# Inverting the triangular matrices of a delta-rule kernel: the first two doubling levels replaced by a back substitution on VectorE

## The chip, the cores and the metric

The kernel runs on one core of a Trainium2 chip. The metric is device time in microseconds of one execution. The medians are taken over several runs; one more execution is recorded by the hardware profiler.

## The reference

The reference is a small network on 512 tokens of width 1024. It has two hybrid layers (a gated delta rule with 8 heads, a windowed attention with 16 query heads and an MLP each) and one further block with a state space branch. The change is in the delta rule. Per head and per chunk of 64 tokens it solves with a unit lower triangular matrix:

```python
L = jnp.where(strict, jnp.einsum('bhnid,bhnjd->bhnij', kb, k) * decay, 0.0)
u = lax.linalg.triangular_solve(L, v * beta[..., None], left_side=True,
                                lower=True, unit_diagonal=True)
w = lax.linalg.triangular_solve(L, kb * jnp.exp(g)[..., None], left_side=True,
                                lower=True, unit_diagonal=True)
# then, chunk after chunk
v_new = u_c - jnp.einsum('bhcd,bhde->bhce', w_c, state)
o = (jnp.einsum('bhcd,bhde->bhce', qd, state) + jnp.einsum('bhij,bhje->bhie', a_c, v_new))
state = state * jnp.exp(gl)[..., None, None] + jnp.einsum('bhcd,bhce->bhde', kd, v_new)
```

All arithmetic is float32.

## The kernel before

**Weights.** Every product with a weight matrix is cut into tiles of 128 output columns by 1024 input rows (`LT_TILES`). A tile is loaded by SyncE, split by ScalarE (L909) and GpSimd (L916) into a high and a low part, and multiplied by TensorE in 24 matmuls of 128x512 (L946 to L948). In the order of work a tile is cut into 8 pieces of three matmuls. The outputs alternate between two PSUM banks, so VectorE has to evict a tile (L1712 for most) before the next but one can start.

**Inverse.** The kernel works with 128x128 blocks, each holding two chunks of 64 tokens; four blocks (`CH`) cover 512 tokens. A block of the transposed matrix lies in `LTm`. `XB` holds, for the lower and the upper 64 partitions, the transposed inverse of each chunk's own 64x64 matrix. It starts from 2x2 diagonal blocks: `first` copies the elements above the diagonal of each 2x2 block from `LTm`, `minus` subtracts them from the unit matrix (L1551, L1553). Then five doubling levels (`LEVELS` = 2, 4, 8, 16, 32) join blocks of that size. A level is a round trip between VectorE and TensorE: `flip` transposes 32x32 blocks of `XB` into `Xi` (L1568), `p` multiplies `LTm` with `Xi` (L1881), `pmask` cuts the result to the off-diagonal blocks of the level (L1572), `q` multiplies again (L1885), and `update` subtracts from `XB` (L1576). Behind the last level `turn`, `plast` and `qlast` join the two chunks of a 128x128 block into `XT`.

**Stages and order.** The work of a layer is a set of chains of stages. Chain D prepares a head: the squares and sums of q and k, the turned copies of k and v, decays, the two Gram products (L1862) and their masking into `LTm` (`maskk`, L1547) and `AT` (`maskq`, L1542). `first` and `minus` are stages of D between `maskk` and `gramq`. D runs through all eight heads one after another, and all its TensorE results go through one PSUM bank, `psD[:, 0]`, which is bank 2. Chain A holds the inverse's levels, head after head. Chains B (two lanes) hold the scan over the chunks. E holds the tiles' evictions and convolutions (`tap3` to `tap0`, `silu`), and C the windowed attention. Each stage waits for the count of its chain's semaphore. Among the waits between chains are these: `tap3` of the q tile of head h waits for the end of D of head h-2, A of a head waits for `minus` of the same head, and the first query tile of the windowed attention (`qraw`) waits for the last head's D and for the scan of the fourth and fifth last head. B of a head needs that head's A and D. Tile `ya` needs all heads.

**Who decides the order.** Each engine executes its instructions in the order in which a small planner (`ordered`, L278) emits the stages. The planner starts the stage that can start earliest by a table of assumed durations (`micros`, L339) times a factor (`slack1`, L375: 1.25 for stages of ScalarE, VectorE and GpSimd of the first six heads). This order is worked out when the kernel is built and is the same in each execution.

Of the kernel before, what the change touches and what calls it, by code (L numbers as in the profile page):

```python
# [9 lines left out]
ALU = mybir.AluOpType  # L10
# [15 lines left out]
SWAP = [i + ROT if i < ROT else i - ROT if i < 2 * ROT else i for i in range(32)]  # L26
LEVELS = (2, 4, 8, 16, 32)
BLK = 64
# [62 lines left out]
for _name, _n in [("ident", P), ("ones", P), ("invfreq", 1), ("isrot", 1), ("signrot", 1), ("notrot", 1),  # L91
                  ("eps", 1), ("eps4", 1), ("halfpi", 1), ("invcount", 16),
                  ("upper", P), ("first", BLK), ("later", P), ("levels", BLK * len(LEVELS)), ("unit", BLK),
                  ("dup0", P), ("dup1", P), ("window", 2 * P)]:
    CONST[_name] = (_at, _at + _n)
    _at += _n
# [22 lines left out]
def constants():  # L119
# [4 lines left out]
    def put(name, v):  # L124
        c[:, CONST[name][0]:CONST[name][1]] = v
# [4 lines left out]
    ib, jb = i % BLK, np.arange(BLK)[None, :]  # L130
    put("first", (ib % 2 == 0) & (jb == ib + 1))
    put("unit", ib == jb)
    put("later", np.where(i <= j, 0.0, NEG))
# [56 lines left out]
def e_stages(tile):  # L190
# [3 lines left out]
    if kind == "f2":  # L194
# [9 lines left out]
D_STAGES = ["square", "sums", "qscale", "turnk", "ksum", "root", "copyk", "turnv", "recip", "dscale", "copyv", "rows", "diff", "exps",  # L204
            "qdec", "gramk", "maskk", "first", "minus", "gramq", "maskq"]

# [132 lines left out]
def micros(e):  # L339
# [13 lines left out]
    if (kind, name) == ("Z", "double"):  # L353
        return (0.5, 1.2, 2.4, 3.0, 4.8, 3.6, 7.2)[int(s[len(name):])]
    special = {("N", "highs"): 2.5, ("N", "adds"): 3.0, ("A", "update"): 0.45, ("A", "turn"): 0.6, ("A", "p"): 1.1, ("A", "q"): 1.1, ("A", "plast"): 0.6, ("A", "qlast"): 0.6,
# [322 lines left out]
def build(nc, xT, pos, consts, gain0, params, weights, params2, smallbc, uD, yD, matsD, lagsD, outT):  # L678

    with ExitStack() as ctx:  # L680
# [92 lines left out]

        scal = sb("scal", [P, HEADS, 8, CH])
        srows = sb("srow", [P, 2, 4, CH])
        DSUM, DROOT, DRECIP, DCOL, DQ = range(5)
# [5 lines left out]
        ps = ctx.enter_context(nc.psum_tensor("ps", [P, 8, 512], F32))  # L782
        psD, psB, psA = ps[:, 2:4, :], ps[:, 4:6, :], ps[:, 6:8, :]
        psS = [ps[:, 4, 0:P], ps[:, 7, 0:P]]
        psO = [ps[:, 5, :], ps[:, 3, :]]
# [132 lines left out]

        def part(layer, earlier):
            names = ("tile_stage", "key_stage", "gate_stage", "gram_stage", "inverse_stage", "scan_even", "scan_odd", "window_even", "window_odd", "mlp_even", "mlp_odd",  # L920
                     "coef_stage", "x_ready", "sq_done", "h_high", "h_low", "ssq_done", "root_done", "rstd_ready", "x_scaled", "post_col", "pre_col", "pre_row",
                     "pre_sum", "sq_added", "post_sum", "coef_in", "sum_done", "post_root", "post_ready", "out_done", "setup", "out_ready", "state_stage", "y_stage",
                     "branch_even", "branch_odd", "mats_out", "mats_even", "mats_odd", "u_out", "u_even", "u_odd", "y_out", "y_in")
            (tile_stage, key_stage, gate_stage, gram_stage, inverse_stage, scan_even, scan_odd, window_even, window_odd, mlp_even, mlp_odd,
             coef_stage, x_ready, sq_done, h_high, h_low, ssq_done, root_done, rstd_ready, x_scaled, post_col, pre_col, pre_row,
             pre_sum, sq_added, post_sum, coef_in, sum_done, post_root, post_ready, out_done, setup, out_ready, state_stage, y_stage,
             branch_even, branch_odd, mats_out, mats_even, mats_odd, u_out, u_even, u_odd, y_out, y_in) = [sem(f"{n}{layer}") for n in names]

# [190 lines left out]

            steps = [0]  # L1120
            MATS_BEFORE, MATS_EACH = 16 * (3 * SG + 2 * SG), 16 * 5
# [145 lines left out]
            if layer < DEPTH:  # L1267
# [219 lines left out]
                def run_vector(v):  # L1487
                    for kind, j, s in L_ORDERS[layer]:
# [5 lines left out]
                        elif kind == "G":  # L1494
# [27 lines left out]
                            ins.then_inc(gate_stage, 1)  # L1522
                        elif kind == "D" and s in ("qscale", "recip", "dscale", "diff", "maskk", "maskq", "first", "minus"):
                            h = j
# [18 lines left out]
                            elif s == "maskk":  # L1543
                                if h >= 3:
                                    v.wait_ge(inverse_stage, A.end(GROUP_OF[h - 3]))
                                for c in range(CH):
                                    ins = v.scalar_tensor_tensor(out=lt[:, c, :], in0=a0[:, c, :], scalar=w[:, DCOL, c:c + 1],  # L1547
                                                                 in1=DT[:, c, :], op0=ALU.mult, op1=ALU.mult)
                            elif s == "first":
                                for b in (lower, upper):  # L1550
                                    ins = v.tensor_tensor(XB[b, (h + 1) % 4, :, :], lt[b, :, b], over_chunks(k_("first")[b], CH, BLK), ALU.mult)  # L1551
                            else:
                                ins = v.tensor_tensor(XB[:, (h + 1) % 4, :, :], over_chunks(k_("unit")), XB[:, (h + 1) % 4, :, :], ALU.subtract)  # L1553
                            ins.then_inc(gram_stage, 1)
# [853 lines left out]
```

## Time and profile before

| | us |
|---|---|
| median of 3 runs | 2500.5 (2500.2 to 2500.54) |
| the profiled execution, device time | 2497.98 |
| its span in the trace | 2496.2 |
| TensorE busy in it | 2414.7 |
| VectorE busy in it | 1266.1 |
| ScalarE busy in it | 1047.8 |
| GpSimd busy in it | 1152.0 |

PE is TensorE's matmuls, PEld its weight loads, DVE VectorE, ACT ScalarE, POOL GpSimd. Times in the trace are microseconds from the start of the span. A float32 matmul of the inverse and of the heads' work appears as two records, so a "p" or "q" step, four blocks by two halves of the partitions, is 16 records. The ends of matmuls are modelled, and a matmul's duration overlaps with the next one's start. The page has the totals; views of groups by line, of stretches of time and of instructions in order of time were read beside it.

### The profile page before, as it was taken

How to read it: one execution, taken by the hardware profiler on the slowest of the kernel's cores; microseconds unless marked ns; L12 is line 12 of the kernel's file. 1: busy time of each engine (PE TensorE's matmuls, PEld its weight loads, DVE VectorE, ACT ScalarE, POOL GpSimd, SP SyncE). 2: the span in 40 equal slices, each digit the busy share in tenths (PEclk: the TensorE clock that was granted, in tenths of full speed). 3: DMA queues.
4: the chain of work that ended last, by engine and by line, in shares of the span. 5: the costliest groups of instructions: out<-in, count | busy, mean ns of one | idle time of the engine just before them, and what ended most of it. 6: DMA issues, size and time to landing. Idle time of an engine off the chain costs nothing.

```text
span 2496.2 us, 35065 instructions
## 1 busy us (share of the span) xinstructions
PE 2414.7 (97%) x13972; PEld 1921.3 (77%) x13972; DVE 1266.1 (51%) x2172; ACT 1047.8 (42%) x2248; POOL 1152.0 (46%) x848
## 2 busy tenths in 40 slices
PE   7999999999999999989999999999999999799998
PEld 5787777778778888767877777787777788677886
DVE  4777744663341111286766446634586511566453
ACT  6565643443343323354656334533533232323342
POOL 4333323335666556543333233256665564433464
PEclk9999999999999999999999999999999999888999
DMA  4211112222323332311111122223133332362322
GB/s 147 60 52 60 52 43 64 65 75 77 101 68 95 100 93 93 101 51 60 60 52 52 43 77 68 60 90 120 61 114 121 120 93 93 112 175 85 101 93 76
DMA packets 76515, 207.48 MB, mean 83 GB/s; under 512 B 16704, under 2 KB 27712, under 8 KB 75840
## 3 DMA queue, kind: packets, MB, share of 16 engines
q1 hardware_dynamic: 76352, 205.24, 26.7%
q8 instruction: 111, 1.82, 0.3%
q14 instruction: 52, 0.43, 0.1%
HBM read 194.72 MB, written 10.49 MB: 82 GB/s over the span
## 4 chain that ended last, share of the span: by engine, by line
PE 83%; DVE 8%; ACT 4%; POOL 2%; issue 2%; DMA 1%; SPq 1%; DVEq 0%; ACTq 0%; POOLq 0%
PE ps L946 24%; PE ps L948 22%; PE ps L947 22%; PE ps L1881 2%; PE ps L1885 2%; PE ps L1934 1%; PE ps L1946 1%; PE ps L1862 1%; ACT wH L909 1%; POOL wL L916 1%; PE ps L1940 1%; DVE ctw L1156 1%; ACT prob L1419 1%; DVE ctmp L1156 1%; PE ps L1911 1%
## 5 line engine op out<-in xcount | busy, mean ns | idle before, releaser
L916 POOL TENSOR_TENSOR wL<-raw,wH 128x512 fp32r<-128x512 f32 x660 | 900.4, 1386 | 1151.7 <-ACT wH L909 1151.4
L909 ACT ACTIVATE wH<-raw 128x512 fp32r<-128x512 f32 x660 | 379.9, 624 | 760.0 <-PE ps L948 756.4
L946 PE MATMUL ps<-hH,wH 128*128 128x512 f32 x1592 | 667.0, 419 | 3.9 <-DVE mixed L2177 2.2
L948 PE MATMUL ps<-hH,wL 128*128 128x512 f32 x1592 | 631.9, 397 | 0.0
L947 PE MATMUL ps<-hL,wH 128*128 128x512 f32 x1592 | 630.0, 396 | 0.0
L946 PEld LDWEIGHTS ps<-hH,wH 128*128 128x128 f32 x1592 | 303.1, 190 | 74.0 <-issue 11.3
L948 PEld LDWEIGHTS ps<-hH,wL 128*128 128x128 f32 x1592 | 302.7, 190 | 67.6
L947 PEld LDWEIGHTS ps<-hL,wH 128*128 128x128 f32 x1592 | 304.2, 191 | 54.0 <-issue 0.5
L946 PE MATMUL ps<-OH,wH 128*128 128x512 f32 x576 | 230.8, 401 | 4.9 <-DVE acc L1741 1.8
L948 PE MATMUL ps<-OH,wL 128*128 128x512 f32 x576 | 227.8, 396 | 0.0
L947 PE MATMUL ps<-OL,wH 128*128 128x512 f32 x576 | 227.8, 395 | 0.0
L946 PE MATMUL ps<-SH,wH 128*128 128x512 f32 x436 | 172.6, 396 | 0.0
L948 PE MATMUL ps<-SH,wL 128*128 128x512 f32 x436 | 172.5, 396 | 0.0
L947 PE MATMUL ps<-SL,wH 128*128 128x512 f32 x436 | 172.4, 395 | 0.0
L946 PEld LDWEIGHTS ps<-OH,wH 128*128 128x128 f32 x576 | 108.2, 188 | 36.8 <-issue 9.2
L1743 DVE TENSOR_TENSOR acc<-acc,ps 128x512 f32<-128x512 f32 x48 | 33.1, 689 | 202.0 <-PE ps L948 202.0
L948 PEld LDWEIGHTS ps<-OH,wL 128*128 128x128 f32 x576 | 108.2, 188 | 26.0
L947 PEld LDWEIGHTS ps<-OL,wH 128*128 128x128 f32 x576 | 108.3, 188 | 24.8
L946 PEld LDWEIGHTS ps<-SH,wH 128*128 128x128 f32 x436 | 81.9, 188 | 20.2 <-issue 0.4
L948 PEld LDWEIGHTS ps<-SH,wL 128*128 128x128 f32 x436 | 81.9, 188 | 19.7
L947 PEld LDWEIGHTS ps<-SL,wH 128*128 128x128 f32 x436 | 81.9, 188 | 19.7
L1419 ACT ACTIVATE prob<-prob,small 128x256 f32<-128x256 f32 (+1 forms) x128 | 59.8, 469 | 61.6 <-DVE small L1657 61.6
(405 smaller groups left out, 3461.3 us busy)
## 6 DMA issues: line engine op xcount, KB each, us to landing
raw<-w SPq DMA_DIRECT2D x345, 512.0 KB, 3.5
mats<-matsD SPq DMA_DIRECT2D x4, 1408.0 KB, 6.7
x<-xT SPq DMA_DIRECT2D x8, 256.0 KB, 5.7
matsD<-Cd SPq DMA_DIRECT2D x8, 256.0 KB, 2.8
matsD<-wide SPq DMA_DIRECT2D x4, 512.0 KB, 3.6
mats<-lagsD SPq DMA_DIRECT2D x32, 64.0 KB, 6.7
outT<-acc SPq DMA_DIRECT2D x8, 256.0 KB, 2.2
matsD<-tab SPq DMA_DIRECT2D x8, 128.0 KB, 1.8
```

What stands on the lines that cost most here:

```text
L909: act.activation(weights_at(slot)[0][:, k, :], raw[:, n % RAW, k, :], ACT.Copy).then_inc(high_done, 1)
L916: pool.tensor_tensor(low[:, k, :], raw[:, n % RAW, k, :], high[:, k, :].bitcast(F32), ALU.subtract).then_inc(low_done, 1)
L946: pe.matmul(out, wh, rH[:, t, :], start=(t == 0), stop=False)
L947: pe.matmul(out, wh, rL[:, t, :], start=False, stop=False)
L948: mm = pe.matmul(out, wl, rH[:, t, :], start=False, stop=(t == depth - 1))
L1156: return v.tensor_tensor(o, a, b, ALU.mult)
L1419: act.activation(prob[:, i, a:], prob[:, i, a:], ACT.Exp, bias=nm4[:, i:i + 1], accum_out=den[:, i:i + 1])
L1743: ins = v.tensor_tensor(acc[:, i % 8, :], acc[:, i % 8, :], b, ALU.add)
L1862: ins = pe.matmul(psD[:, 0, cc], k[:, cc], (k if s == "gramk" else q)[:, cc], start=True, stop=True)
L1881: ins = pe.matmul(psA[b, 0, cc], lt[b, c, b], Xi[b, i, :], start=True, stop=True)
L1885: ins = pe.matmul(second_half(psA[b, 0, cc], n), Pm[b, i, :], second_half(xb[b, i, :], n), start=True, stop=True)
L1911: ins = pe.matmul(psS[e], XT[SLOT[h]][:, c, :], vb[SLOT[h]][:, 0, :] if c == 0 else rr, start=True, stop=True)
```

## The change

The levels 2 and 4 are left out: `LEVELS` is now (8, 16, 32), and the inverse starts from 8x8 diagonal blocks (`PACK` = 8) that VectorE inverts.

- `first` now copies all elements above the diagonal of each 8x8 block of `LTm` into `XB` (the mask is another one, the two instructions are the same).
- `pack` sums the eight column groups of `XB` into a packed array of 4 x 8 elements per partition: only the own group isn't zero. The packed array lies in PSUM, in the bank of `psD[:, 0]`.
- Six stages `solve6` to `solve1` do the substitution. Each one copies row k of every 8x8 block to the block's eight partitions (a shuffle of the partitions), multiplies it with column k and subtracts the product. The three instructions depend on each other; `solve_link` makes VectorE wait for its own last instruction through the new semaphore `solve_step`.
- `minus` subtracts the packed array from the unit matrix, and a second instruction spreads it into `XB` with the mask `group`.

The new stages belong to chain D, between `first` and `minus`; the planner's table has 0.4 us for `pack`, 0.5 for a `solve` and 0.6 for `minus` (0.45 before). The semaphores of a part of the program that it doesn't use are no longer allocated. The core of the diff:

```diff
-LEVELS = (2, 4, 8, 16, 32)
+PACK = 8
+LEVELS = (8, 16, 32)
...
-    put("first", (ib % 2 == 0) & (jb == ib + 1))
-    put("unit", ib == jb)
+    put("first", (ib // PACK == jb // PACK) & (jb > ib))
+    put("unit", ib % PACK == np.arange(PACK)[None, :])
+    put("group", ib // PACK == jb // PACK)
...
-            "qdec", "gramk", "maskk", "first", "minus", "gramq", "maskq"]
+            "qdec", "gramk", "maskk", "first", "pack"] + [f"solve{k}" for k in range(PACK - 2, 0, -1)] + [
+    "minus", "gramq", "maskq"]
...
-               ("D", "first"): 0.9, ("D", "minus"): 0.45, ("B", "v"): 0.25, ("B", "r"): 0.7,
+               ("D", "first"): 0.9, ("D", "pack"): 0.4, ("D", "solve"): 0.5, ("D", "minus"): 0.6, ("B", "v"): 0.25, ("B", "r"): 0.7,
...
+        solve_rows = sb("solve_rows", [P, 2, CH * PACK])
...
+        packed = ps[:, 2, 0:CH * PACK]
...
-            steps = [0]
+            steps, solved = [0], [0]
+
+            def solve_link(v, ins):
+                solved[0] += 1
+                ins.then_inc(solve_step, 1)
+                v.wait_ge(solve_step, solved[0])
...
+                            elif s == "pack":
+
+                                ins = v.tensor_reduce(packed.rearrange("p (c r) -> p c r", r=PACK),
+                                                      XB[:, (h + 1) % 4, :, :].rearrange("p c (g r) -> p c r g", r=PACK), AX.X, ALU.add)
+                            elif s.startswith("solve"):
+
+                                k = int(s[5:])
+                                rows, prod = (solve_rows[:, i, :].rearrange("p (c r) -> p c r", r=PACK) for i in range(2))
+                                V = packed.rearrange("p (c r) -> p c r", r=PACK)
+                                solve_link(v, v.stream_shuffle(solve_rows[:, 0, :], packed, [p // PACK * PACK + k for p in range(32)]))
+                                solve_link(v, v.tensor_tensor(prod, V[:, :, k:k + 1].to_broadcast([P, CH, PACK]), rows, ALU.mult))
+                                ins = v.tensor_tensor(V, V, prod, ALU.subtract)
                             else:
-                                ins = v.tensor_tensor(XB[:, (h + 1) % 4, :, :], over_chunks(k_("unit")), XB[:, (h + 1) % 4, :, :], ALU.subtract)
+                                V = packed.rearrange("p (c r) -> p c r", r=PACK)
+                                solve_link(v, v.tensor_tensor(V, k_("unit").unsqueeze(1).to_broadcast([P, CH, PACK]), V, ALU.subtract))
+                                in_groups = lambda m: m.rearrange("p c (g r) -> p c g r", r=PACK)
+                                ins = v.tensor_tensor(in_groups(XB[:, (h + 1) % 4, :, :]),
+                                                      V.unsqueeze(2).to_broadcast([P, CH, BLK // PACK, PACK]),
+                                                      k_("group").rearrange("p (g r) -> p g r", r=PACK).unsqueeze(1).to_broadcast(
+                                                          [P, CH, BLK // PACK, PACK]), ALU.mult)
```

## Rows read from the trace of the kernel before

**Rows 1.** The page, busy time and share of each engine.

```profile
PE 2414.7 (97%) x13972; PEld 1921.3 (77%) x13972; DVE 1266.1 (51%) x2172; ACT 1047.8 (42%) x2248; POOL 1152.0 (46%) x848
```

**Rows 2.** The page, chain that ended last, shares by engine.

```profile
PE 83%; DVE 8%; ACT 4%; POOL 2%; issue 2%; DMA 1%; SPq 1%; DVEq 0%; ACTq 0%; POOLq 0%
```

**Rows 3.** Stretches: length, busy PE, PEld, DVE, ACT, POOL (instructions), granted clock, DMA, GB/s.

```profile
82.00:339.00 257.00, 254.56 (x2185) 202.40 (x2184) 184.16 (x381) 152.29 (x365) 86.21 (x63) 0.99 0.17 52
339.00:417.00 78.00, 77.75 (x623) 61.29 (x623) 27.62 (x67) 25.05 (x66) 23.94 (x20) 1.00 0.18 55
...
270.00:300.00 30.00, 29.43 (x237) 22.96 (x236) 24.47 (x44) 22.22 (x50) 11.74 (x8) 1.00 0.22 70
```

**Rows 4.** Groups by line: the levels' steps; busy us, mean ns, idle before.

```profile
L1881 PE MATMUL ps<-Xi,LTm 64*64 64x64 f32 x1280 | 54.5, 224 | 0.1
L1885 PE MATMUL ps<-XB,Pm 64*64 64x32 f32 x1280 | 52.4, 222 | 0.4 <-DVE Pm L1572 0.3
```

**Rows 5.** TensorE in order of time: start us, us, line, operation, records.

```profile
158.78 0.39 PE L947 MATMUL ps<-hL,wH 128*128 128x512 f32 x1
159.01 0.40 PE L948 MATMUL ps<-hH,wL 128*128 128x512 f32 x1
159.34 0.68 PE L1881 MATMUL ps<-Xi,LTm 64*64 64x64 f32 x16
159.95 0.50 PE L946 MATMUL ps<-hH,wH 128*128 128x512 f32 x1
160.28 0.39 PE L947 MATMUL ps<-hL,wH 128*128 128x512 f32 x1
...
294.30 0.68 PE L1881 MATMUL ps<-Xi,LTm 64*64 64x64 f32 x16
294.91 0.49 PE L1909 MATMUL ps<-S,ks 128*128 128x128 f32 x2
```

**Rows 6.** Groups by line and form: flip, masking and update of the levels.

```profile
L1568 DVE STREAM_TRANSPOSE Xi<-XB 128x256 f32<-128x256 f32 x80 | 35.0, 438 | 1.6
L1572 DVE TENSOR_TENSOR Pm<-ps,cst 128x256 f32<-128x256 f32 x80 | 33.7, 421 | 48.0 <-PE ps L1881 47.3
L1576 DVE TENSOR_TENSOR XB<-XB,ps 128x128 f32<-128x128 f32 x80 | 22.6, 283 | 21.3 <-PE ps L1885 20.9
```

**Rows 7.** The same view: minus, and the nearest forms to the added instructions.

```profile
L1553 DVE TENSOR_TENSOR XB<-cst,XB 128x256 f32<-128x256 f32 x16 | 11.1, 693 | 0.1
...
L1649 DVE TENSOR_REDUCE small<-prob 128x2 f32<-128x256 f32 x16 | 6.6, 410 | 0.0
...
L1626 DVE STREAM_SHUFFLE rstdp<-qraw 128x512 f32<-128x512 f32 x8 | 6.0, 754 | 0.0
...
L1659 DVE TENSOR_TENSOR small<-small 128x4 f32<-128x4 f32 x32 | 5.7, 177 | 13.4 <-ACT small L1421 13.4
```

**Rows 8.** VectorE and ScalarE in order of time, layer 0.

```profile
81.76 0.69 DVE L1542 TENSOR_TENSOR AT<-ps,DT 128x512 f32<-128x512 f32 x1 [0.29 <-PE ps L1862]
84.09 0.71 ACT L1447 ACTIVATE qs<-tmp,par 128x512 f32<-128x512 f32 x1
...
262.83 0.69 DVE L1542 TENSOR_TENSOR AT<-ps,DT 128x512 f32<-128x512 f32 x1 [0.68 <-PE ps L1862]
...
286.43 0.71 ACT L1447 ACTIVATE qs<-tmp,par 128x512 f32<-128x512 f32 x1
...
306.24 0.69 DVE L1542 TENSOR_TENSOR AT<-ps,DT 128x512 f32<-128x512 f32 x1 [0.79 <-PE ps L1862]
306.96 0.63 ACT L1351 ACTIVATE sq<-qs 128x512 f32<-128x512 f32 x1
...
339.15 0.69 DVE L1542 TENSOR_TENSOR AT<-ps,DT 128x512 f32<-128x512 f32 x1 [0.65 <-PE ps L1862]
...
358.89 0.69 DVE L1712 TENSOR_TENSOR qraw<-ps,rstd 128x512 f32<-128x512 f32 x1 [3.39 <-POOL OL L1290]
...
422.34 0.68 DVE L1712 TENSOR_TENSOR gate<-ps,rstd 128x512 f32<-128x512 f32 x1
```

**Rows 9.** VectorE in order of time: an instruction and its dependent.

```profile
1828.69 0.17 DVE L1207 TENSOR_SCALAR small<-small 128x16 f32<-128x16 f32 x1
1828.90 0.35 DVE L1156 TENSOR_TENSOR small<-small 128x16 f32<-128x16 f32 x3
```

More of the change, by code:

```diff
@@ L92 @@
                   ("eps", 1), ("eps4", 1), ("halfpi", 1), ("invcount", 16),
-                  ("upper", P), ("first", BLK), ("later", P), ("levels", BLK * len(LEVELS)), ("unit", BLK),
+                  ("upper", P), ("first", BLK), ("later", P), ("levels", BLK * len(LEVELS)), ("unit", PACK), ("group", BLK),
                   ("dup0", P), ("dup1", P), ("window", 2 * P)]:
@@ L919, in part @@
         def part(layer, earlier):
+            FIRST_BLOCK = ("gate_stage", "key_stage", "gram_stage", "inverse_stage", "scan_even", "scan_odd", "window_even", "window_odd", "mlp_even",
+                           "mlp_odd", "coef_stage", "coef_in", "setup", "mats_out", "solve_step")
+            SECOND_BLOCK = ("out_done", "out_ready", "state_stage", "y_stage", "branch_even", "branch_odd", "mats_even", "mats_odd", "u_out",
+                            "u_even", "u_odd", "y_out", "y_in")
             names = ("tile_stage", "key_stage", "gate_stage", "gram_stage", "inverse_stage", "scan_even", "scan_odd", "window_even", "window_odd", "mlp_even", "mlp_odd",
@@ L922, in part @@
                      "pre_sum", "sq_added", "post_sum", "coef_in", "sum_done", "post_root", "post_ready", "out_done", "setup", "out_ready", "state_stage", "y_stage",
-                     "branch_even", "branch_odd", "mats_out", "mats_even", "mats_odd", "u_out", "u_even", "u_odd", "y_out", "y_in")
+                     "branch_even", "branch_odd", "mats_out", "mats_even", "mats_odd", "u_out", "u_even", "u_odd", "y_out", "y_in", "solve_step")
             (tile_stage, key_stage, gate_stage, gram_stage, inverse_stage, scan_even, scan_odd, window_even, window_odd, mlp_even, mlp_odd,
@@ L926, in part @@
              pre_sum, sq_added, post_sum, coef_in, sum_done, post_root, post_ready, out_done, setup, out_ready, state_stage, y_stage,
-             branch_even, branch_odd, mats_out, mats_even, mats_odd, u_out, u_even, u_odd, y_out, y_in) = [sem(f"{n}{layer}") for n in names]
+             branch_even, branch_odd, mats_out, mats_even, mats_odd, u_out, u_even, u_odd, y_out, y_in, solve_step) = [sem(f"{n}{layer}") if n not in (FIRST_BLOCK if layer == DEPTH else SECOND_BLOCK) else None for n in names]
             def lane(tile):
@@ L1522, in run_vector @@
                             ins.then_inc(gate_stage, 1)
-                        elif kind == "D" and s in ("qscale", "recip", "dscale", "diff", "maskk", "maskq", "first", "minus"):
+                        elif kind == "D" and s in ("qscale", "recip", "dscale", "diff", "maskk", "maskq", "first", "pack", "minus") or kind == "D" and s.startswith("solve"):
                             h = j
```

## The prediction

> **What bounds the kernel now.** I read the page first. TensorE is busy for 2414.7 of 2496.2 us, VectorE for 51% [rows 1], and the chain of work that ended last runs through TensorE for 83% of its length, with VectorE at 8% [rows 2]. So a microsecond taken from TensorE's own instructions is worth about a microsecond, as long as the other engines deliver on time. Then I read the stretches in which the inverses are made. In layer 0 this is 82 to 339 us: TensorE is busy for 254.56 of 257 us at a granted clock of 0.99, VectorE for 184.16, or 72%. In the 78 us behind it TensorE is busy for 77.75 and VectorE for 27.62. The fullest VectorE slice that I looked at inside the heads' stretch holds 24.47 of 30 us (82%), and TensorE is still busy for 29.43 there [rows 3]. Layer 1 repeats the pattern. TensorE does not wait for the inverse: it runs weight tiles between the inverse's steps, in an order fixed beforehand. The inverse is dear because its steps occupy TensorE.
>
> **What is removed on TensorE.** Two of five levels, each with a "p" and a "q" step per head: 2 x 2 x 16 heads = 64 steps of 16 records. The records agree: 1280 + 1280 on the two lines, two fifths of which are 1024 = 64 x 16. They are busy for 54.5 + 52.4 us, two fifths of it 42.8 us [rows 4]. Busy time overlaps with neighbours, so I price a step by starts. One that stands alone between wide matmuls: the wide one before starts at 159.01, the second wide one behind at 160.28, which is 1.27 us, and two wide matmuls take 0.23 us each when they follow each other (158.78 to 159.01): 1.27 - 0.46 = 0.81 us. One that has another narrow group behind it: 294.30 to 294.91, 0.61 us [rows 5]. Since both kinds are common I take 0.72. 64 x 0.72 = 46 us; the ends are 64 x 0.61 = 39 and 64 x 0.81 = 52. TensorE is full here, so this comes off the span: 23 us per layer, 2.9 us per head.
>
> **What is removed on VectorE.** Per head, twice a flip (438 ns), a masking (421) and an update (283): 2 x 1.142 = 2.28 us [rows 6].
>
> **What is added on VectorE.** Per head "pack", six "solve" steps of three instructions, and "minus" as two instead of one. None of these forms is in the trace: VectorE writes PSUM nowhere. The pack reads 256 elements per partition; a reduction of that size takes 410 ns. A shuffle of 512 elements takes 754 ns. The slope between 256 and 512 elements is about 1.04 ns per element (421 ns for 256 in the masking [rows 6], 690 for the maskq of 512 [rows 8]), so for 32 elements the shuffle is 754 - 480 x 1.04 = 255 ns. A tensor-tensor of 4 elements takes 177 ns [rows 7], with 28 elements more 0.2 us. Each instruction that depends on the one before waits for its own semaphore. Such a link costs little: one ends at 1828.69 + 0.17 = 1828.86 and its dependent starts at 1828.90, a gap of 0.04 us [rows 9]. A solve step is 0.255 + 0.2 + 0.2 + 3 x 0.04 = 0.78 us, six are 4.7. The pack is 0.45. The new minus is 0.2 + 0.04 + 0.42 = 0.66 against 0.693 for the old one [rows 7]: nothing. The old one reads two SBUF tensors and is stretched from 421 ns, the time of the masking of equal size with a PSUM operand [rows 6], to 693 on average; all added instructions have at most one SBUF tensor, so I stretch none of them. Added: 5.1 us per head. Net for VectorE: 5.1 - 2.3 = +2.8 us per head, 45 us in all. Below, the six steps cost no less than 18 x 0.177 = 3.2 us; above, if writing and rereading PSUM costs as much again as the instruction, 8 us.
>
> [...]
>
> **Where the added work lies.** VectorE has 184.16 / 7 = 26.3 us of work in each of the seven head periods between 82 and 339 us, which are 36.8 us long. That becomes 29.1 us in 36.8 - 2.9 = 33.9: 86%. This is above the 82% that the trace shows beside a full TensorE [rows 3], so some waits will appear. More important is the order. Stage chain D is one chain through all heads: the square of a head starts 0.03 us after the last mask of the head before has ended (306.24 + 0.69, then 306.96), and from the first head's maskq end at 82.45 to the last one's at 339.84 its period is 36.8 us [rows 8]. All 5.1 us lie on it. Queued behind the solve steps on VectorE are the evictions of weight tiles, the taps of the convolution and the scan's steps; behind "minus" stands "gramq" in TensorE's queue. Two things absorb this. The q tile of head h+2 waits for head h: at first there are 1.6 us between (82.45, 84.09), with the sixth head 22.9 (263.52, 286.43), so weight tiles lag ever further behind chain D. And the query tiles of the window part need the last head's D, which is done at 339.84, while the first of them is scaled at 358.89, where it waited for the scan [rows 8]. With TensorE 21 us earlier by then, that cushion is gone: its turn is at 338 against a D end near 340. So I charge stalls. Nothing is late if D shrinks with TensorE's queue as the other chains do; 6 us per layer is my choice, worked out as 0.75 us in each of eight heads, about one turn of a weight-tile piece (three wide matmuls, 0.7 us) lost per head. The other level chain, A, gets two round trips per head shorter, so the scan behind it is not late. The constants' load is 120 columns shorter and the new semaphore adds no other wait; I cost both at nothing, since the masks are loaded while the first tiles run.
>
> **Sum.** -46 + 12 = -34 us. The profiled execution took 2497.98 us with a span of 2496.2; its device time goes to 2464. The median of the runs is 2500.5, 2.5 above it, so the forecast for the median is 2466.5 us. With its own ends: 2450 (52 saved, no stall) to 2476.
>
> **The rivals.** (1) *Chain D eats half.* If 2.4 of the 5.1 us per head aren't absorbed, D ends 19 us later, at 359, and the window's query tiles start where they start today. What lies behind them is shorter, because chain A no longer lags: today 63.4 us pass from 358.89 to the first gate at 422.34 [rows 8], of which eight tiles of 24 wide matmuls are 8 x 24 x 0.23 = 44 us; the rest of A and the scan is then some 10. That gains 9 us per layer: 2482. For it: D is already continuous. Against: its period is 36.8 us of which TensorE's fixed order makes most, and that order is shortened.
> (2) *Chain D sets the pace, slower than before.* If nothing is absorbed, D ends 8 x 5.1 = 41 us later, at 381 us. The first window tile is then scaled at 381, the first gate at 381 + 54 = 435, 13 us later than today: 2500.5 + 26 = 2527. It decides from (41 - 13) / 8 = 3.5 us per head that isn't absorbed. For it: the same continuity, and the cushion of 1.6 us at the first head. Against: while TensorE is full, a wait in D is a turn in its queue and not latency, and there are fewer steps in that queue now.
> (3) *The small instructions on PSUM are dearer than the rows near them.* 19 of them per head; at 0.5 us each instead of 0.25 VectorE has 29.1 + 4.8 = 33.9 us of work in 33.9, and TensorE waits for evictions. At that point the gain is about used up: 2500.
>
> **How the numbers follow.** Forecast 60%, rival 1 20%, rival 2 13%, rival 3 and other ways to no change 7%. The 80% range runs from 2450 to 2494: it takes in the forecast's own range and rival 1 with its surroundings, and leaves out rival 2 and 3. A measurement of this kernel can tell about 0.2%, 5 us, from no change. Faster by more than that 0.80, within it 0.07, slower 0.13.
>
> **What would show it.** The "p" and "q" lines with 768 records each instead of 1280; TensorE busy some 43 us shorter and as full between the heads as now. The three instructions of a solve within 0.8 us; if over 1.2, rival 3. The period of maskq near 34 us; if 37 or more, rivals 1 or 2, and then TensorE shows idle time before the wide matmuls of the tiles behind q, released by VectorE's evictions. The first window tile scaled near 338 to 345. The prediction is wrong if TensorE's idle time grows by more than 20 us in all.

## The result, and the profile after

The changed kernel takes 2532.6 us (median of 4 runs, 2531.4 to 2534.1) against 2500.5 for the kernel before in the same comparison: the ratio is 1.0126, 95% interval 1.0108 to 1.0143. It is 32 us slower, where 34 us faster was forecast, and outside the range of 2450 to 2494. The profiled execution has a span of 2532.3 us, 36.1 more than before.

The page of the changed kernel, busy time of each engine and the chain that ended last:

```profile
PE 2416.4 (95%) x12948; PEld 1917.3 (76%) x12948; DVE 1278.6 (50%) x2492; ACT 1045.1 (41%) x2246; POOL 1148.8 (45%) x848
...
PE 79%; DVE 11%; ACT 4%; POOL 2%; issue 2%; DMA 1%; SPq 0%; DVEq 0%; ACTq 0%; POOLq 0%
```

TensorE executes 1024 matmul records fewer than in [rows 1], and is busy for 1.7 us more. Its idle time is 2532.3 - 2416.4 = 115.9 us against 2496.2 - 2414.7 = 81.5. So 34.4 us of the 36.1 are new idle time, and the rest of the question is why fewer matmuls take as long. Stretches answer this (columns as in [rows 3]):

```profile
82.00:339.00 257.00, 241.73 (x1699) 192.52 (x1698) 180.22 (x485) 139.74 (x335) 83.73 (x61) 0.92 0.16 52
339.00:417.00 78.00, 72.46 (x538) 57.58 (x537) 35.91 (x123) 31.41 (x88) 17.75 (x16) 0.91 0.13 41
...
205.00:220.00 15.00, 14.87 (x84) 12.85 (x85) 11.22 (x44) 4.67 (x12) 5.75 (x6) 1.00 0.32 103
220.00:230.00 10.00, 7.77 (x89) 6.07 (x88) 8.95 (x20) 9.29 (x25) 2.30 (x2) 0.71 0.16 53
...
224.00:224.50 0.50, 0.46 (x3) 0.46 (x4) 0.50 (x2) 0.47 (x2) 0.00 (x0) 0.76 1.04 393
224.50:225.00 0.50, 0.50 (x3) 0.10 (x1) 0.50 (x2) 0.00 (x0) 0.00 (x0) 0.50 0.88 360
...
225.00:230.00 5.00, 3.23 (x37) 2.58 (x36) 4.14 (x10) 4.91 (x14) 0.00 (x0) 0.50 0.00 1
```

In the heads' stretch TensorE is now idle for 15.3 of 257 us (2.4 before), and its mean granted clock is 0.92 instead of 0.99; in the 78 us behind it is 0.91 instead of 1.00. VectorE is not fuller than before in the heads' stretch: 180.22 us against 184.16. The groups by line and form (busy us, mean ns, idle before) show each new instruction:

```profile
L1914 PE MATMUL ps<-Xi,LTm 64*64 64x64 f32 x768 | 36.6, 242 | 5.6 <-DVE Xi L1601 5.4
L1918 PE MATMUL ps<-XB,Pm 64*64 64x32 f32 x768 | 34.2, 232 | 4.3 <-DVE Pm L1605 4.3
...
L1562 DVE SCALAR_TENSOR_TENSOR LTm<-ps,scal,DT 128x128 f32<-128x128 f32 x64 | 18.0, 345 | 24.4 <-PE ps L1895 24.4
...
L1569 DVE TENSOR_REDUCE ps<-XB 128x32 f32<-128x256 f32 x16 | 10.7, 669 | 0.2
...
L1576 DVE STREAM_SHUFFLE solve_rows<-ps 128x32 f32<-128x32 f32 x96 | 18.5, 192 | 0.0
L1577 DVE TENSOR_TENSOR solve_rows<-ps,solve_rows 128x32 f32<-128x32 f32 x96 | 18.4, 192 | 3.3
L1578 DVE TENSOR_TENSOR ps<-ps,solve_rows 128x32 f32<-128x32 f32 x96 | 19.1, 199 | 3.3
```

The first two are the "p" and "q" steps of [rows 4], with 768 records each. They had 0.1 and 0.4 us of idle time before them, now 5.6 and 4.3. Of the four lines below, L1569 is the pack and L1576 to L1578 are a solve step. L1562 is `maskk`, which waited 4.7 us for the Gram product before (at L1547) and waits 24.4 now. The waits of TensorE (total us, times, longest) have a new entry that the prediction had named as the sign of its rivals: wide matmuls that wait for the eviction of a tile behind the q tile.

```profile
PE ps L955 <- DVE tmp L1745: 8.5, 7, 1.7
```

With the two level lines (5.5 and 3.9 us more than before) this is 17.9 of the 34.4 us of new idle time; the rest is spread over many lines.

VectorE and ScalarE in order of time, to be laid beside [rows 8] (L1557 is maskq, L1462 a first tap, `gate` the first tile behind the query tiles):

```profile
89.85 0.69 DVE L1557 TENSOR_TENSOR AT<-ps,DT 128x512 f32<-128x512 f32 x1 [0.77 <-PE ps L1895]
92.80 0.71 ACT L1462 ACTIVATE qs<-tmp,par 128x512 f32<-128x512 f32 x1
...
376.14 0.69 DVE L1557 TENSOR_TENSOR AT<-ps,DT 128x512 f32<-128x512 f32 x1 [1.56 <-PE ps L1895]
384.39 0.69 DVE L1745 TENSOR_TENSOR qraw<-ps,rstd 128x512 f32<-128x512 f32 x1 [1.27 <-ACT vtok L1475]
...
438.93 0.68 DVE L1745 TENSOR_TENSOR gate<-ps,rstd 128x512 f32<-128x512 f32 x1
```

Chain D's period is (376.14 - 89.85) / 7 = 40.9 us instead of 36.8. It ends 37.0 us later, the first query tile is scaled 25.5 us later, and the first gate tile 16.6 us later. Layer 1 repeats this: its first gate tile comes at 1504.92 instead of 1475.43, another 12.9 us.

Where TensorE loses the time is seen behind the end of a head's D. TensorE in order of time (bracket: idle before, releaser):

```profile
219.50 1.06 PE L1895 MATMUL ps<-qs,ks 128*128 128x128 f32 x8
...
225.30 1.12 PE L1914 MATMUL ps<-Xi,LTm 64*64 64x64 f32 x16 [0.30 <-DVE Xi L1601]
226.60 1.11 PE L1938 MATMUL ps<-cst,osq 128*128 128x128 f32 x4 [0.18 <-DVE osq L1635]
227.64 1.07 PE L1918 MATMUL ps<-XB,Pm 64*64 64x32 f32 x16
230.05 0.77 PE L955 MATMUL ps<-hH,wH 128*128 128x512 f32 x1 [1.34 <-DVE tmp L1745]
```

L1914 is a "p" step: 1.12 us, where [rows 5] shows 0.68. The granted clock of 225 to 230 us is 0.50, which is the lower of the two levels, 1.2 GHz. The stretch from 220 to 230 us has not one matmul of L955. The same view of L955 alone, of the changed kernel (first fence) and of L946 of the kernel before (second):

```profile
205.00:220.00 15.00, 6.44 (x15) 2.84 (x15) 1.00 0.32 103
220.00:230.00 10.00, 0.00 (x0) 0.00 (x0) 0.71 0.16 53
```

```profile
205.00:220.00 15.00, 4.88 (x11) 2.08 (x11) 1.00 0.28 80
220.00:230.00 10.00, 2.95 (x8) 1.23 (x7) 1.00 0.11 43
```

Before, weight tile pieces stand between the narrow steps. Now they are spent while D is busy with its solve steps. The head's remaining narrow steps then follow one another with waits, and the clock halves: within 224.00 to 224.50 us, by the stretches above. The whole executions agree: the granted clock of the whole execution is 0.960 here, 0.978 in e1 and 0.981 in e2 below, which execute the same matmuls.

### The profile page after: what moved, and what is told of

Same layout as the page of the kernel before. It is cut to its first block, busy times and chain, and to the rows that moved or that the text cites. A ratio compares the mean times of both kernels' runs of the same rounds, so it can differ in the third digit from the quotient of the medians.

```text
span 2532.3 us, 33335 instructions
## 1 busy us (share of the span) xinstructions
PE 2416.4 (95%) x12948; PEld 1917.3 (76%) x12948; DVE 1278.6 (50%) x2492; ACT 1045.1 (41%) x2246; POOL 1148.8 (45%) x848
## 4 chain that ended last, share of the span: by engine, by line
PE 79%; DVE 11%; ACT 4%; POOL 2%; issue 2%; DMA 1%; SPq 0%; DVEq 0%; ACTq 0%; POOLq 0%
PE ps L955 23%; PE ps L957 22%; PE ps L956 22%; PE ps L1895 1%; PE ps L1967 1%; PE ps L1979 1%; POOL wL L921 1%; ACT wH L914 1%; DVE ctw L1171 1%; PE ps L1973 1%; PE ps L1914 1%; ACT prob L1434 1%; PE ps L1918 1%; DVE ctmp L1171 1%; PE ps L1929 1%
## 5 line engine op out<-in xcount | busy, mean ns | idle before, releaser
L955 PE MATMUL ps<-hH,wH 128*128 128x512 f32 x1592 | 669.3, 420 | 12.5 <-DVE tmp L1745 8.5
L956 PE MATMUL ps<-hL,wH 128*128 128x512 f32 x1592 | 637.6, 401 | 0.0
L955 PEld LDWEIGHTS ps<-hH,wH 128*128 128x128 f32 x1592 | 305.2, 192 | 87.7 <-issue 20.6
L955 PE MATMUL ps<-OH,wH 128*128 128x512 f32 x576 | 230.8, 401 | 4.6 <-DVE acc L1774 1.8
L955 PE MATMUL ps<-SH,wH 128*128 128x512 f32 x436 | 172.6, 396 | 0.0
L955 PEld LDWEIGHTS ps<-OH,wH 128*128 128x128 f32 x576 | 108.2, 188 | 36.5 <-issue 8.9
L955 PEld LDWEIGHTS ps<-SH,wH 128*128 128x128 f32 x436 | 81.9, 188 | 20.1 <-issue 0.4
```

What stands on the lines that cost most here:

```text
L955: pe.matmul(out, wh, rH[:, t, :], start=(t == 0), stop=False)
L956: pe.matmul(out, wh, rL[:, t, :], start=False, stop=False)
```

## The experiments

The expectations set these theories against each other. L: the loss is the latency of pack, solve and minus on chain D. V: it is VectorE's load. T: TensorE's work remains the bound. C (in e1's expectation alone): other waits make the shorter work on TensorE worth nothing. O (from the second group on): it is the order that the planner works out once it has seven stages more in D. "After" is the changed kernel. All medians below were compared with runs of the kernel before on the same chip (2500.4 to 2505.3 us).

### The placement, the work and the load

**e1_moved.** Pack, solve and minus are taken from D and put at the front of chain A; the packed array lies in another bank.

```diff
-            "qdec", "gramk", "maskk", "first", "pack"] + [f"solve{k}" for k in range(PACK - 2, 0, -1)] + [
-    "minus", "gramq", "maskq"]
+            "qdec", "gramk", "maskk", "first", "gramq", "maskq"]
...
-A_STAGES = (["flipi"] + ...
+A_STAGES = (["pack"] + [f"solve{k}" for k in range(PACK - 2, 0, -1)] + ["minus", "flipi"] + ...
...
-        packed = ps[:, 2, 0:CH * PACK]
+        packed = ps[:, 6, CH * BLK:CH * BLK + CH * PACK]
```

> The changed kernel with pack, the six solve stages and minus moved out of chain D to the front of chain A; the packed array moves to an unused part of A's own PSUM bank. Same instructions, same work for VectorE and TensorE. Theory L (the latency on chain D paces the stage): D gets shorter than in the kernel before (no minus in it), its period falls from 40.9 us to 36 or less, TensorE is full again at a granted clock near 1.0: 2455 to 2475 us. Theory V (VectorE's load, 29 us per head, is the bound): the load is the same, so the time stays within 10 us of 2532. Theory C (shorter TensorE work makes no difference because of other waits): about 2500.

Measured: 2470.2 us, ratio 0.9873 (0.9858 to 0.9889). That is 30 us below the kernel before and 62 below after, with the same instructions on TensorE and VectorE as after. Its page line, its heads' stretch, and VectorE in order of time (L1565 is `first`, L1556 maskq):

```profile
PE 2380.5 (96%) x12948; PEld 1888.2 (76%) x12948; DVE 1294.7 (52%) x2492; ACT 1052.8 (43%) x2254; POOL 1153.7 (47%) x848
```

```profile
82.00:339.00 257.00, 249.27 (x1878) 199.35 (x1878) 203.83 (x535) 157.39 (x378) 89.19 (x64) 0.99 0.16 54
```

```profile
218.92 0.85 DVE L1565 TENSOR_TENSOR XB<-LTm,cst 64x256 f32<-64x256 f32 x2
...
222.84 0.69 DVE L1556 TENSOR_TENSOR AT<-ps,DT 128x512 f32<-128x512 f32 x1
...
336.31 0.69 DVE L1556 TENSOR_TENSOR AT<-ps,DT 128x512 f32<-128x512 f32 x1 [0.70 <-PE ps L1895]
344.14 0.69 DVE L1745 TENSOR_TENSOR qraw<-ps,rstd 128x512 f32<-128x512 f32 x1 [1.81 <-PE ps L956]
...
407.04 0.68 DVE L1745 TENSOR_TENSOR gate<-ps,rstd 128x512 f32<-128x512 f32 x1
```

VectorE is busy for 203.83 of 257 us here, more than in after or before, and the kernel is the faster one: V is false. The other bank was not tried by itself; the solve instructions cost the same in both (191 to 199 ns each here, 192 to 199 in after). D ends at 337, the first query tile is scaled at 344.14 and the first gate comes 15.3 us earlier than in [rows 8]. Against after, the same 12948 records are busy for 35.9 us less and idle time is 27.3 us less (88.6 against 115.9). The two add up to the 63.2 us between the spans. The granted clock of the run is 0.978 against 0.960. So I put the longer busy time, somewhat more than half of the loss against e1, down to matmuls executed at the lower clock; the rest is waits.

**e2_no_solve.** The six solve stages are left out, from the kernel and from the planner's list; pack and minus stay in D.

```diff
-"first", "pack"] + [f"solve{k}" for k in range(PACK - 2, 0, -1)] + [
+"first", "pack"] + [] + [
```

> The changed kernel without the six solve stages (18 small VectorE instructions per head); pack and minus stay. The substitution is left out. Theory L: D loses about 4 us per head against the changed kernel, its period falls from 40.9 to about 37, near that before: 2475 to 2500 us. Theory V: VectorE loses 3.5 us per head, also 2470 to 2500, so this run tells the size and not which of the two. If the time stays above 2520, it is neither, but the rest of D (the pack of 669 ns) or the planner's order.

Measured: 2464.2 us, ratio 0.9846 (0.983 to 0.9862). D's period is 36.0 us. Without the two levels, and with D hardly longer, the time falls by 36 us: the forecast's TensorE term is sound as long as D isn't lengthened.

**e3_double_p.** The "p" matmuls are executed twice, 48 steps more on TensorE.

```diff
-    ins = pe.matmul(psA[b, 0, cc], lt[b, c, b], Xi[b, i, :], start=True, stop=True)
+    for again in range(2):
+        ins = pe.matmul(psA[b, 0, cc], lt[b, c, b], Xi[b, i, :], start=True, stop=True)
```

> The changed kernel with each matmul of the p steps issued twice, the same result written again: 48 more steps' worth of TensorE work, about 29 us at 0.6 us each, unknown to the planner. Theory L: TensorE waits for D in these stretches, so most of the added work falls into waits, and a fuller TensorE may keep its clock: the time rises by less than 15 us or even falls (2515 to 2547). Theory T (TensorE's own work still sets the time, and the loss is from elsewhere): +29 us and more, above 2560.

Measured: 2539.5 us, ratio 1.0153 (1.0135 to 1.017), only 7 us above after for 48 steps, which at the prediction's 0.61 us each are 29 us. The planner's prices are untouched, so the order is that of after. T is false: TensorE has room in the changed kernel. The room is of two kinds. The "p" records are busy for 64.0 us instead of 36.6, 27.4 more, but all of TensorE for only 13.4 more (2429.8 against 2416.4), at a granted clock of 0.966 instead of 0.960: the other matmuls got 14 us shorter. And idle time fell by 8.6 us, from 115.9 to 107.3.

**e4_before_plus_solve.** The kernel before, with all five levels, and an idle pack and six idle solve stages in D, between `first` and `minus`.

```diff
-            "qdec", "gramk", "maskk", "first", "minus", "gramq", "maskq"]
+            "qdec", "gramk", "maskk", "first", "pack"] + [f"solve{k}" for k in range(6, 0, -1)] + ["minus", "gramq", "maskq"]
...
```

> The kernel before, all five levels kept, with pack and the six solve stages added to D between first and minus as idle work whose result isn't used. Theory L: D grows as in the changed kernel and TensorE still has its 64 steps; D paces, so the steps cost little more: 2535 to 2560 us. Theory T (TensorE's work sets the time and the added instructions hide beside it): 2500 to 2510, and the changed kernel's loss would come from something that only it has (the three-level chain A or minus).

Measured: 2544.6 us, ratio 1.0171 (1.0147 to 1.0195), D's period 40.6 us. So the stages in D cost the kernel before 44 us. From here, leaving out the two levels is worth 2544.6 - 2532.6 = 12 us (both figures hold another order in them, see below). Without the solves in D it is worth 36 (e2). The saving on TensorE shrinks once D sets the pace, as e3 shows from the other side.

### The instructions' latency, or the order

**e5_order_only.** The planner counts the six stages, so the order on TensorE, ScalarE, GpSimd and SyncE is that of after (the two traces have the same 12948 matmul records in the same order), but their 18 instructions per head are not executed.

```diff
-D = Count([(h, D_STAGES) for h in range(HEADS)])
+D = Count([(h, D_STAGES) for h in range(HEADS)], ("solve",))
...
```

> The changed kernel with the planner still counting the six solve stages, so that TensorE, ScalarE and GpSimd have exactly the changed kernel's order, but without the 18 instructions. The substitution is left out. Theory L (the time that the instructions take on chain D): D is short in fact, 2465 to 2480 us, near the 2464 of the run whose planner didn't count them. Theory O (the order that the planner makes with the longer D is what costs): near 2532.

Measured: 2527.6 us, ratio 1.0104 (1.0088 to 1.0119). Leaving out 96 solve steps with their latency gains 5 us of the 68 that lie between after and e2. Its page line, then TensorE (gramk and gramq) and VectorE in order of time; L1566 is `first`, L1581 and L1583 are `minus`, L1557 is maskq:

```profile
PE 2412.2 (95%) x12948; PEld 1915.5 (76%) x12948; DVE 1223.9 (48%) x2108; ACT 1043.7 (41%) x2246; POOL 1151.0 (46%) x848
```

```profile
203.03 1.16 PE L1895 MATMUL ps<-ks 128*128 128x128 f32 x8 [0.43 <-POOL qd L1300]
...
217.40 1.06 PE L1895 MATMUL ps<-qs,ks 128*128 128x128 f32 x8
```

```profile
205.53 0.85 DVE L1566 TENSOR_TENSOR XB<-LTm,cst 64x256 f32<-64x256 f32 x2
...
215.55 0.35 DVE L1622 SCALAR_TENSOR_TENSOR S<-S,small,ps 128x128 f32<-128x128 f32 x1 [2.70 <-PE ps L1946]
215.81 0.19 DVE L1581 TENSOR_TENSOR ps<-cst,ps 128x32 f32<-128x32 f32 x1
216.03 0.42 DVE L1583 TENSOR_TENSOR XB<-ps,cst 128x256 f32<-128x256 f32 x1
...
218.50 0.69 DVE L1557 TENSOR_TENSOR AT<-ps,DT 128x512 f32<-128x512 f32 x1 [0.19 <-PE ps L1895]
```

Nothing but the pack (0.68 us) has to be done between 206.4 and 215.8, and yet `minus` starts there. In VectorE's emitted order it stands behind a step of the scan (L1622), for which VectorE waits 2.70 us, since that step's matmul (L1946) stands behind weight pieces in TensorE's order. On TensorE gramq stands 14.4 us behind gramk, with or without the instructions: in after the pair starts at 205.13 and 219.50. D's period is 40.5 us. Pure L is false. e2 and e5 execute the same instructions; TensorE is busy for 2412.2 against 2374.6 us, and idle for 114.1 against 88.5 us. The granted clock of the run is 0.961 against 0.981. That is 37.6 us of longer matmuls plus 25.6 of waits, 63 us in all, made by the order alone.

**e6_plan_free.** The opposite: all is executed, but the planner's table has next to nothing for it.

```diff
-("D", "pack"): 0.4, ("D", "solve"): 0.5, ("D", "minus"): 0.6,
+("D", "pack"): 0.05, ("D", "solve"): 0.01, ("D", "minus"): 0.45,
```

> The changed kernel, all instructions in place, with the planner told that pack and solve cost next to nothing (0.05 and 0.01 us instead of 0.4 and 0.5; minus 0.45 instead of 0.6); only the order changes. Theory O: the order returns to that of a kernel with a short D, 2465 to 2490 us. Theory L: the latency is there whatever the order, and TensorE now meets D's steps too early and waits for them with everything behind: 2525 to 2560.

Measured: 2530.4 us, ratio 1.0117 (1.01 to 1.0134), D's period 40.7 us; from the start of `first` to that of maskq it is 10.6 us on average over layer 0's heads (12.3 in after, 12.0 in e5, 5.8 in e2, 5.3 before). Telling the planner less doesn't help: then the instructions' own latency, about 5 us, and what VectorE does between them fill the gap. So O holds for the changed kernel as it is. For this one L is argued from the 4.8 us by which that way is longer than in e2; its order isn't e2's either, so no run separates the two here. Planned or not, the work is paid for in D.

**e7_half.** Three solve stages instead of six.

```diff
-[f"solve{k}" for k in range(PACK - 2, 0, -1)]
+[f"solve{k}" for k in range(PACK - 2, PACK - 5, -1)]
```

> The changed kernel with three of the six solve stages. Half of the substitution is left out. Between 2464 us without and 2532 with all six. Theory L with a fixed cost per microsecond of D: halfway, 2490 to 2505. If D only costs above a threshold (hidden behind TensorE's queue up to some length), the first three stages are cheap: below 2485.

Measured: 2497.8 us, ratio 0.9983 (0.9974 to 0.9993), period 39.2 us: midway between e2 and after (2498.4).

**e8_fused and e9_fused_priced.** The six solve stages become one stage of D, priced 3.9 us in the planner's table (e8) or 3.2 (e9, with 0.55 for pack and 0.5 for minus).

```diff
-    k = int(s[5:])
+    for k in range(PACK - 2, 0, -1):
+        if k < PACK - 2:
+            solve_link(v, ins)
...
```

> The changed kernel with the six solve stages made one stage of 3.9 us, so that no other VectorE instruction gets between them. Same instructions. In the changed kernel some 12 us pass from first to maskq against 5 before, of which pack and solve are 5; the rest is foreign work let in between. Theory L: D gets 1 to 3 us per head shorter, the other VectorE work waits up to 4 us more at a time: 2500 to 2525 us. Theory O: the time depends on the planner's luck, no direction.

> Nothing of the computation is left out. The kernel after with its six solve stages as one stage of chain D, as in e8_fused, and this stage priced in the planner's table as the trace of the kernel after shows it: pack 0.55 us, solve 3.2, minus 0.5 (e8_fused had 3.9 for the solve and gave 2516). Theory O (the emitted order makes the loss; the instructions' time is small): the shorter price lets the planner hold gramq and the later stages less far back; 2495 to 2512, D period 38 to 39 us. Theory L (the loss is the real latency of pack, solve and minus on chain D): the price changes nothing, 2514 to 2520, D period as in e8_fused.

Measured: 2516.1 us, ratio 1.0053 (1.0038 to 1.0068), and 2505.5 us, ratio 1.0023 (1.0012 to 1.0034). In both VectorE executes the same instructions in D as in after, in one go; `first` to maskq takes 10.1 and 9.9 us. So up to 17 to 27 us of the loss may come from drawing the six steps apart; each is one order against one other, and the runs below show that orders alone differ by as much.

**e10_moved_fused.** e1 with the fused stage, priced as in e9.

> Nothing of the computation is left out. The placement of e1_moved (pack, solve and minus at the front of chain A, packed array in the bank of the inverse's products), with the six solve stages as one, priced 3.2 us, pack 0.55, minus 0.5. With the work off chain D both theories expect the period of maskq at 36 us and a time near that of e1_moved. Theory O: fewer separate stages, so less is drawn apart by the planner, 2460 to 2472. Theory L: 2465 to 2475, since the latency in chain A is the same. Above 2480 would say that the order's details are worth as much as the placement.

Measured: 2504.7 us, ratio 1.0009 (0.9999 to 1.0019). This is a miss: 34 us above e1, no better than e9, and D's period in layer 0 is 41.0 us though nothing was added to D. In layer 1 it is 35.5 us, as in e1. The first gate of layer 0 comes 24 us later than in e1 (430.90 against 407.04) and that of layer 1 35 us later (1476.11 against 1441.49). One stage of 3.2 us in chain A gives another order of everything. With the fused stage the placement in A is thus worth nothing at this setting. So how far the order alone moves the time had to be measured before the placement could be judged.

### How much is any order worth

In these runs only the planner's factor for the first six heads is 1.2 or 1.3 instead of 1.25; the instructions stay the same.

```diff
-        f = 0.9 if last_heads else 1.25
+        f = 0.9 if last_heads else 1.3
```

> Nothing of the computation is left out. The kernel before with one number of the planner changed: the factor on the assumed durations of ScalarE, VectorE and GpSimd stages of the first six heads is 1.3 instead of 1.25. The instructions are the same, only their order differs. This measures how much the time moves by the order alone, without any change in the work. Theory O expects a movement that can be measured, slower, since the order before was fitted to the kernel before: 2503 to 2520. Theory L (latency and work alone make the time): 2498 to 2503.

> Nothing of the computation is left out. The kernel after with the same one number changed, 1.3 instead of 1.25. If the loss of the kernel after is a property of the particular order that the planner found for it (bad luck, which another setting would not repeat), this run moves by more than 10 us to either side of 2532, and may come near 2500. If it is the placement of the eight stages in chain D that forces it, 2525 to 2545.

> Nothing of the computation is left out. The kernel before, planner's factor 1.2 instead of 1.25, order alone changed. e11 (1.3) gave 2522.8. If the order of the kernel before is a chosen good one among similar ones, this is again slower: 2508 to 2530. If 1.3 was an outlier: 2498 to 2506.

> Nothing of the computation is left out. The kernel after, factor 1.2 instead of 1.25. e12 (1.3) gave 2542.5. If the placement of the eight stages in chain D costs time under any order, this stays 2525 to 2545, and above the kernel before with the same factor by 15 us or more. If the loss is only the order that was found at 1.25, it moves to 2490 to 2520.

> Nothing of the computation is left out. e1_moved (pack, solve and minus at the front of chain A) with the factor 1.2. e1_moved gave 2470.2 at 1.25. If the placement is what matters, this stays below the kernel before with the same factor by 15 us or more, 2465 to 2500. If e1_moved was a lucky order, 2500 to 2530.

> Nothing of the computation is left out. e1_moved with the factor 1.3. Same reading as for 1.2: below the kernel before with 1.3 (2522.8) by 15 us or more if the placement is what matters, 2470 to 2505; near or above it, 2510 to 2540, if e1_moved was a lucky order.

> e2_no_solve with the factor 1.2: the six solve stages are left out, from the kernel and from the planner's table, pack and minus stay in chain D; the inverse is wrong, the work of all other parts is the same. e2 gave 2464.2 at 1.25. If the six extra stages in chain D carry the loss under any order: 2465 to 2490, below the kernel after with the same factor (2533.9) by 45 us or more. If e2 was a lucky order: 2495 to 2525.

> e2_no_solve with the factor 1.3: the six solve stages are left out as in e17. If the six extra stages in chain D carry the loss under any order: 2465 to 2495, below the kernel after with the same factor (2542.5) by 45 us or more. If e2 was a lucky order: 2495 to 2525.

Medians, us (in the comparisons that they were run in, the kernel before at 1.25 gave 2500.4 to 2505.3; the runs of the column 1.2 without e17 share one chip with e16, as do e11 and e12 another):

| kernel | 1.2 | 1.25 | 1.3 | mean |
|---|---|---|---|---|
| before | 2523.3 | 2500.5 | 2522.8 | 2515.5 |
| after (stages in D) | 2533.9 | 2532.6 | 2542.5 | 2536.3 |
| e1 (stages in A) | 2477.4 | 2470.2 | 2496.3 | 2481.3 |
| e2 (no solve stages) | 2473.5 | 2464.2 | 2472.4 | 2470.0 |

Three things follow. First, the kernel before is at an order that suits it: either neighbour is slower by 18 and 20 us against the kernel before measured beside it (ratios 1.0073 and 1.0081, lower ends 1.0058 and 1.0062). Second, at each factor after is slower than before (by 11, 32 and 20 us) and e1 faster (by 46, 30 and 26). With six separate stages, D against A is worth 46 to 62 us in each pair. Third, the six stages in D cost 66 us in the mean (2536.3 - 2470.0), in A 11 (2481.3 - 2470.0); the 11 hold a gain as well, since e1 takes pack and minus out of D too and e2 doesn't. About 21 of the 32 us of the result are left in the mean over three orders; the rest is that before's order at 1.25 is a good one.

Left open: why the fused stage in A (e10) lengthens D in layer 0, and whether it would do better at other factors. Not tried: a third buffer for q and v, which would let tiles run further ahead of D. The clock's share was not taken by itself: the 36 to 38 us above are read from busy times of equal instructions beside the granted clock, and e3, which fills some narrow stretches with more matmuls, shows part of it coming back.

## Why the prediction was wrong

**The bound.** The views were read rightly: TensorE bounds the kernel before. That this stays so was assumed; after the change D sets the pace (e3, e4).

**Removed from TensorE: right.** 43 us of busy time and 46 by starts were forecast. The means over three orders give 2420.9 us busy before (2414.7, 2424.5, 2423.4) and 2378.0 in e2 (2374.6, 2379.9, 2379.5): 42.9. The mean times are 45.5 us apart.

**Added to VectorE: size right in sum.** A solve step of the changed kernel in order of time:

```profile
123.28 0.19 DVE L1576 STREAM_SHUFFLE solve_rows<-ps 128x32 f32<-128x32 f32 x1
123.51 0.19 DVE L1577 TENSOR_TENSOR solve_rows<-ps,solve_rows 128x32 f32<-128x32 f32 x1
123.73 0.20 DVE L1578 TENSOR_TENSOR ps<-ps,solve_rows 128x32 f32<-128x32 f32 x1
```

It takes 123.93 - 123.28 = 0.65 us where 0.78 was forecast; the shuffle is 192 ns, not 255. The pack is 669 ns, where the nearest row gave 410. That is 0.26 us more for 256 elements, and no run separates what makes it: the pack reads elements 8 apart, has 32 sums instead of 2, and writes to PSUM. The Trainium skill ("Vector Engine (DVE) Microarchitecture Reference", section 5.2 "Measured stream behaviour on trn2") has 1.71 to 2.51 ns per column for streams that step at every element, against 1.054 for contiguous ones, though not for one source stepping by 8 words. By estimate from it the step alone would add 0.17 to 0.37 us, and the measured 0.26 lies between. Six steps and the pack come to 6 x 0.65 + 0.67 = 4.6 us against 5.1. Rival 3 was false: the 18 small instructions take 0.19 to 0.20 us each, not 0.5. The net was too high all the same: VectorE's busy time grew by 12.5 us in after (1278.6 against 1266.1) and by 28.6 in e1 (1294.7), where 45 were forecast. The 5.1 us per head had the gaps of the links in them, which are no busy time.

**Where the added work lies: the step that failed.** The prediction saw that all 5.1 us lie on D, that the cushion of 1.6 us at the first head and that of the window's query tiles would be gone, and then charged 6 us per layer, "about one turn of a weight-tile piece lost per head". Its reason was that a wait in D is a turn in TensorE's queue, and that the order is only shortened. The order is not given: it is worked out anew with seven stages more, each priced and stretched by 1.25. From `first` to maskq D now takes 12.3 us instead of 5.3, though the instructions between have grown by only 4.6 us less 0.05 for minus, and e5 shows that they needn't even be executed. D's period became 40.9 us instead of the forecast 34, and TensorE's idle time grew by 34.4 us instead of 12.

**The clock: not in the sum.** The prediction priced stalls by their length. Here a head alternates between a stretch in which TensorE runs weight pieces and the scan's groups but no level step, and one with narrow dependent steps; in the head shown above, and in some others, the clock falls to 0.50 in the latter. A "p" step then costs 1.12 / 0.68 = 1.65 times as much. Against e2 that is 2416.4 - 2374.6 = 41.8 us in after, as much as the removed steps had been worth.

**The sum by its terms,** in profiled spans: -40.1 for the removed records (2374.6 in e2 against 2414.7), +41.8 for equal records at a lower clock, +34.4 for idle time: +36.1.

**The rivals.** Rival 2, with a chance of 13%, is what happened: it had D's end at 381 us (measured 376.83), the first window tile at 381 (384.39), the first gate at 435 (438.93), and 2527 in all (2532.6). Its decision point of 3.5 us per head not absorbed was passed: D ends 37.0 / 8 = 4.6 us per head later. Its reason was incomplete: it had only the latency, and leaving that out with the order kept gains 5 us (e5). That its total comes so near is thus in part luck. I gave it too little because I took the fixed order as evidence for the forecast; it was the part most sure to change. The forecast's numbers are met by e1: the first window tile within 338 to 345 (344.14), and 2470.2 us against 2466.5. That is one order of three, the neighbours give 2477.4 and 2496.3. Of the signs that the prediction had named, the period of maskq, the wait for evictions behind the q tile and the idle time all pointed to rival 2.

## What to carry to other kernels

Before a stage is added to a planned kernel, ask which chain it joins: here six separate stages cost some 11 us in a chain with slack and 66 in the one that serves all heads in turn, while fused into one they cost about 40 in either (e9, e10), for a reason left open. Where a planner emits the order, an edit of the stage list changes the order of everything; rerun the kernel before at neighbouring settings of the planner to learn how much an order alone is worth (here 1 to 26 us between neighbouring settings), and put that into the range. A saving on the full engine counts only while that engine stays fed, and here the waits between narrow matmuls went with a lower clock, which cost about as much as the waits themselves.

## What the runs showed of the hardware

The granted clock fell to 0.50 between 224.00 and 224.50 us. From 219.50 us to the fall there was not one wide matmul, and the longest single wait of TensorE was 0.25 us. A "p" step took 1.12 us instead of 0.68 then. I had not expected a fall without a long wait. The wide matmuls behind it, from 230.05 us, still took 0.63 us each (the first one 0.77); from 234.91 us on they took 0.40 again. Small VectorE instructions that read or write PSUM cost 190 to 199 ns for 32 elements, and a dependent one starts 0.04 us behind the one it waits for (at 123.51, behind 123.28 + 0.19 = 123.47), so chains of them are cheap. Sums over 256 elements 8 apart, 32 of them and into PSUM, took 669 ns, against 411 for two sums of neighbouring ones into SBUF.
